# High and low parts of x side by side in one 512 column matmul, in passes of 256 output columns

## What is computed

```python
n = rmsnorm(h)                       # 256 x 2048
u = n @ w_in                         # A 6144, B 6144, C 10304 columns, gates 6144
# A: b * conv3(c * hid)              each 2048 wide
# B: stick-breaking attention        16 heads of 128, q, k, v
# C: z, xbc, dt = split(u_c); xbc = silu(conv4(xbc) + bias)
#    xdt = x * dt; W = exp(min(cs_l - cs_s, 0)) * (c b) lower half; y = W xdt + exp(cs) * c * state
#    y = (y + d * x) * silu(z); y = y * rsqrt(mean(y*y over a group)) * norm_w
h = h + (g_a*(y_a@w_a) + g_b*(y_b@w_b) + g_c*(y_c@w_c)) @ w_out
h = h + experts(rmsnorm(h))          # 16 of 16384 single-neuron experts for each of 8 heads
return rmsnorm(h, final_norm_w)
```

## Time and profile before

| | us |
|---|---|
| median of 3 runs | 3534.88 (3530.73 to 3535.65) |
| the profiled execution | 3526.34 |
| its span in the trace | 3524.6 |
| mean granted clock of PE | 0.997 |
| PE busy | 98% of the span |
| VectorE, ScalarE busy | 64%, 49% |
| start | 0 to 18.1 |
| A, its branch stage | 18.1 to 310.6, to 494.0 |
| B, its branch stage | to 812.9, to 993.0 |
| C, its branch stage | to 1512.0, to 1791.6 |
| output projection | to 1898.3 |
| expert stages | to 3512, end 3524.6 |

### The profile page before, as it was taken

How to read it: one execution, slowest core, us unless ns; L and a number is a source line. 1 busy time by engine, 2 the same in 40 slices (tenths; PEclk the granted TensorE clock), 3 DMA queues, 4 the chain that set the end, 5 groups by cost and what they waited for, 6 DMA issues and landing times.

```text
span 3524.6 us, 69345 instructions
## 1 busy us (share of the span) xinstructions
PE 3442.4 (98%) x23037; PEld 3164.8 (90%) x23037; DVE 2254.7 (64%) x2944; ACT 1717.8 (49%) x2494; POOL 26.3 (1%) x32
## 2 busy tenths in 40 slices
PE   8999999999999999999989999999999999999998
PEld 7999889998899999978879999999999988888887
DVE  4555444444547777774545998988889855554555
ACT  4444434444445455454435444447777644444444
POOL 0000000000000000000000000000000000000000
PEclk9999999999999999999999999999999999999999
DMA  6666665556666556556668576665666677667765
GB/s 179 175 176 176 187 179 157 158 157 178 193 188 189 174 168 186 172 155 194 188 190 209 158 171 177 175 175 160 158 160 159 166 195 192 193 193 219 197 192 166
DMA packets 484120, 628.63 MB, mean 178 GB/s; under 512 B 76832, under 2 KB 341504, under 8 KB 481792
## 3 DMA queue, kind: packets, MB, share of 16 engines
q1 hardware_dynamic: 483648, 626.51, 65.0%
q10 hardware_dynamic: 320, 0.08, 0.0%
HBM read 622.03 MB, written 4.26 MB: 178 GB/s over the span
## 4 chain that ended last, share of the span: by engine, by line
PE 81%; DVE 7%; DMA 4%; issue 3%; ACT 3%; SPq 2%; DVEq 0%; ACTq 0%
PE bank L81 26%; PE bank L82 25%; PE bank L83 25%; DMA w_raw<-in_peer_down 2%; DVE f_lo L128 2%; PE bank L1766 2%; PE bank L2176 2%; DVE w_lo L1617 1%; DVE c_xc L1200 1%; DMA f_raw<-in_w_in 1%; ACT f_hi L123 1%; SPq L458 1%; SPq L552 1%; DMA f_raw<-in_w_out 0%; SPq L465 0%
## 5 line engine op out<-in xcount | busy, mean ns | idle before, releaser
L128 DVE TENSOR_TENSOR f_lo<-f_raw,f_hi 128x768 fp32r<-128x768 f32 (+2 forms) x640 | 748.5, 1173 | 716.8 <-ACT f_hi L123 716.2
L123 ACT ACTIVATE f_hi<-f_raw 128x768 fp32r<-128x768 f32 (+2 forms) x640 | 646.2, 1016 | 752.1 <-DMA f_raw<-in_w_in 505.7
L81 PE MATMUL bank<-xT_hi,f_hi 128*128 128x256 f32 x2560 | 738.7, 289 | 26.9 <-DVE f_lo L128 12.0
L82 PE MATMUL bank<-xT_lo,f_hi 128*128 128x256 f32 x2560 | 723.9, 283 | 0.0
L83 PE MATMUL bank<-xT_hi,f_lo 128*128 128x256 f32 x2560 | 723.9, 283 | 0.0
L81 PE MATMUL bank<-xT_hi,w_hi 128*128 128x256 f32 x2048 | 587.4, 287 | 9.8 <-DVE w_lo L1617 9.6
L82 PE MATMUL bank<-xT_lo,w_hi 128*128 128x256 f32 x2048 | 579.1, 283 | 0.0
L83 PE MATMUL bank<-xT_hi,w_lo 128*128 128x256 f32 x2048 | 579.1, 283 | 0.0
L1704 DVE TENSOR_TENSOR w_lo<-w_raw,w_hi 128x1024 fp32r<-128x1024 f32 x256 | 313.7, 1225 | 340.1 <-PE bank L83 333.1
L81 PEld LDWEIGHTS bank<-xT_hi,f_hi 128*128 128x128 f32 x2560 | 490.2, 191 | 42.1 <-DVE f_lo L128 15.6
L82 PEld LDWEIGHTS bank<-xT_lo,f_hi 128*128 128x128 f32 x2560 | 490.5, 192 | 1.9 <-issue 1.7
(11 more groups left out here) (274 smaller groups left out, 4833.4 us busy)
## 6 DMA issues: line engine op xcount, KB each, us to landing
w_raw<-in_peer_down SPq DMA_DIRECT2D x1024, 128.0 KB, 3.4
w_raw<-in_peer_up SPq DMA_DIRECT2D x1024, 128.0 KB, 2.6
f_raw<-in_w_in SPq DMA_DIRECT2D x1024, 96.0 KB, 2.4
f_raw<-in_w_in SPq DMA_DIRECT2D x256, 256.0 KB, 2.9
f_raw<-in_w_in SPq DMA_DIRECT2D x384, 128.0 KB, 2.8
f_raw<-in_w_branch_c SPq DMA_DIRECT2D x256, 128.0 KB, 2.8
f_raw<-in_w_branch_a SPq DMA_DIRECT2D x128, 128.0 KB, 2.8
f_raw<-in_w_branch_b SPq DMA_DIRECT2D x128, 128.0 KB, 2.8
```

The source lines that it names most:

```text
L81: nc.tensor.matmul(out, lhs[0], rhs[0], start=start, stop=False, skip_group_check=True)
L82: nc.tensor.matmul(out, lhs[0], rhs[1], start=False, stop=False, skip_group_check=True)
L123: nc.scalar.activation(self.hi[u % 4][:, 0:cols], self.raw[u % 4][:, 0:cols], ACT.Copy).then_inc(self.hi_done, 1)
L128: nc.vector.tensor_tensor(self.lo[u % 4][:, 0:cols], self.raw[u % 4][:, 0:cols], self.hi[u % 4][:, 0:cols].bitcast(F32), ALU.subtract).the ...
```

## The change

**Operands.** `xT_hi` and `xT_lo` become the two halves of one tile `xT` [128, 2, 16, 256]. `pair_matmul` takes the place of `tri_matmul` in A, C and for q and k in B: one matmul of the high weights with 512 moving columns (256 of x high, 256 of x low) into a whole bank, then one of the low weights with the 256 high columns into the bank's first half. The result of 128 output columns is the sum of the two halves. The v part of B keeps its three matmuls.

**Passes.** A unit is now 4 contraction blocks x 256 columns (a 128 x 1024 slot), and four units make a pass: 256 finished output columns in two banks (`pass_unit`, 16 matmuls). A and B have 12 units an iteration (3 passes), C has 20 (x, x, B and C, z, z). `pass_load` issues four DMAs of 32 partitions, in runs of 1 KB (in pass 2 of C two for B, two for C, in runs of 512 B); SP's ring rules are as before.

**Sums.** Two units behind the end of a pass ScalarE copies the second halves of its banks out (`part_a`, `part_qk`, `part_c`), one unit later VectorE adds the first halves (`sum_a`, `sum_qk`, `sum_c`). PE waits for these sums before it starts a pass in the same banks. Passes use banks 0 to 5 in A, 0 to 3 (and 4 for v) in B, and in C 4, 2, 3, 0, 1 in turn.

**Steps moved.** In C the convolution of a group is made within its own iteration, its first tap by ScalarE (`taps`); the clamp min(., 0) goes from VectorE (8 instructions an iteration) to ScalarE (16 of 128 x 128, as a Relu of the negative, on which `exp_w` works in one instruction for a chunk); `xc` is doubled, and the loop over C covers two iterations. The steps stand so ("n" is the iteration's own group, others are of the one before, "r" of the one before that):

| step of C | before, unit | after, unit |
|---|---|---|
| ACT copies | 0 (five) | n: 6, 10, 14, 18; last pass: 2 (two each) |
| DVE sums | none | n: 7, 11, 15, 19; last pass: 3 |
| DVE convolution of block 0 to 5 | 0 to 5 | n: 9, 10, 13, 14, 17, 18 (ACT taps n: 8, 12, 16) |
| ACT silu of x, of z | 6, 7 | 0, 4 |
| clamp, first and second chunk | DVE 10, 12 | ACT n: 17; 1 |
| exponent of cs; of the weights (ACT) | 9; 10, 12 | n: 19; 5 |
| DVE tokens (`c_xdt`, `c_xdd`, `c_cbm`) | 8 | 4 |
| DVE weights | 12, 13 | 6 |
| PE turn, states, outputs | 6, 12, 13 | 0, 4, 8 |
| DVE skip and gate; fold | 15; r: 0 | 12; 15 |
| PE `square_sum` | r: 1 | 14 |
| DVE normalise; low part of y | r: 6; 7 | r: 0; 7 |
| SP `cs_load` | 4, of the group before | 13, of its own |

The rest follows from this: x is turned for six block pairs, not two, before unit 0 of A; unit u < 4 of the first iteration waits for the low part of x's blocks 4u to 4u+3; in the branch stages the accumulators use other bank pairs, the dt step bank 3, and in B's the low part of the last heads waits in a few places for `b_olo`. The text of the output projection and the expert stages stays, save for a semaphore that takes over another's counts.

```diff
+A_PASS = ((1, 0, 1), (2, 2, 3), (0, 4, 5))
+C_BANK = (4, 2, 3, 0, 1, 4, 2, 3, 0, 1)
...
-        xT_hi = sb(top, "xT_hi", [P, KD, T], F32R)
-        xT_lo = sb(top, "xT_lo", [P, KD, T], F32R)
+        xT = sb(top, "xT", [P, 2, KD, T], F32R)
+        xT_hi, xT_lo = xT[:, 0, :, :], xT[:, 1, :, :]
+
+        def pair_matmul(out, lhs, k, start, stop):
+            both = out[:, :].rearrange("p (s t) -> p s t", s=2)
+            nc.tensor.matmul(both, lhs[0], xT[:, :, k, :], start=start, stop=False, skip_group_check=True)
+            return nc.tensor.matmul(both[:, 0, :], lhs[1], xT_hi[:, k, :], start=False, stop=stop,
+                                    skip_group_check=True)
...
-        A_N, B_N, C_N = 128, 128, 128
+        A_N, B_N, C_N = 96, 96, 160
...
-        W, UN, N_IT = 1280, 16, GROUPS
+        W, UN, N_IT = 1024, 20, GROUPS
         zs = place("c_zs", [P, 4, T], at_s)
-        xc = place("c_xc", [P, 6, T], at_s + 4096)
+        xc = (place("c_xc0", [P, 6, T], at_s + 4096), place("c_xc1", [P, 6, T], at_s + 43648))
...
+                def pass_load(n, i, cols, rows):
+                    for q in (3, 2, 1, 0):
+                        at = slice(32 * q, 32 * q + 32)
+                        sp.dma_start(fl.raw[i][at, 0:1024].rearrange("p (k n) -> p k n", k=4)[:, :, cols],
+                                     rows.rearrange("(k p) n -> p k n", p=P)[at, :, :]).then_inc(fl.raw_full[i], 16)
...
-                def evacuate_a(p):
-                    act.wait_ge(fl.used, U_AB * p + U_AB)
-                    nc.scalar.activation(c_sb[:, :], bank[1][:, :], ACT.Copy).then_inc(a_evac, 1)
-                    nc.scalar.activation(b_sb[:, :], bank[0][:, :], ACT.Copy).then_inc(a_evac, 1)
+                def part_a(p, r):
+                    act.wait_ge(fl.used, U_AB * p + 4 * r + 4)
+                    for j in range(2):
+                        dst = (c_sb[:, j * T:(j + 1) * T], gate_hid[:, j, 2:T + 2], b_sb[:, j * T:(j + 1) * T])[r]
+                        if r == 1 and first_p(p) and j == 0:
+                            act.wait_ge(a_pad, 1)
+                        nc.scalar.activation(dst, bank[A_PASS[r][1 + j]][:, T:2 * T], ACT.Copy).then_inc(a_part, 1)
...
+                def taps(p, e, b):
+                    for j in (b, b + 1):
+                        act.wait_ge(ssd["evac"], 10 * p + j + 1)
+                        ch = 4 * p + j if j < 4 else (32 + p if j == 4 else 40 + p)
+                        nc.scalar.activation(xc[e][:, j, :], xpad[:, j, 3:T + 3], ACT.Identity,
+                                             bias=vcols[:, ds(V_CONVB + ch, 1)],
+                                             scale=vcols[:, ds(V_SSDW + 144 + ch, 1)]).then_inc(ssd["tap"], 1)
...
+                def clamp(p, ch):
+                    act.wait_ge(ssd["cs_in"], 16 * p + 16)
+                    if ch:
+                        act.wait_ge(ssd["ecs"], p + 1)
+                    for h in range(HPG):
+                        here = wts[:, ch, h, :]
+                        nc.scalar.activation(here, here, ACT.Relu, bias=cs_col[:, ch, ds(HPG * p + h, 1)],
+                                             scale=-1.0).then_inc(ssd["clamp"], 1)
+
                 def exp_w(p, ch):
-                    for q in range(2):
-                        act.wait_ge(ssd["min"], 4 * p + 2 * ch + q + 1)
-                        here = wts[:, ch, 4 * q:4 * q + 4, :]
-                        nc.scalar.activation(here, here, ACT.Exp).then_inc(ssd["exp"], 1)
+                    act.wait_ge(ssd["clamp"], 2 * HPG * p + HPG * (ch + 1))
+                    nc.scalar.activation(wts[:, ch, :, :], wts[:, ch, :, :], ACT.Exp, scale=-1.0).then_inc(ssd["exp"], 1)
...
+                        if u == 18:
+                            inv_rms(p)
...
+                def sum_a(p, r):
+                    for j in range(2):
+                        here = (c_sb[:, j * T:(j + 1) * T], gate_hid[:, j, 2:T + 2], b_sb[:, j * T:(j + 1) * T])[r]
+                        dve.wait_ge(a_part, 6 * p + 2 * r + j + 1)
+                        nc.vector.tensor_tensor(here, here, bank[A_PASS[r][1 + j]][:, 0:T], ALU.add).then_inc(a_sum, 1)
...
+                def sum_c(p, r):
+                    for j in (2 * r, 2 * r + 1):
+                        here = xpad[:, j, 3:T + 3] if r < 3 else zs[:, j - 6, :]
+                        dve.wait_ge(ssd["part"], 10 * p + j + 1)
+                        nc.vector.tensor_tensor(here, here, bank[C_BANK[j]][:, 0:T], ALU.add).then_inc(ssd["evac"], 1)
...
+                        if u == 15:
+                            fold(p)
...
+                def pass_unit(i, banks):
+                    for kk in range(4):
+                        k = 4 * i + kk
+                        for b in range(2):
+                            at = slice(kk * 256 + b * P, kk * 256 + b * P + P)
+                            last = pair_matmul(banks[b], (fl.hi[i][:, at], fl.lo[i][:, at]), k,
+                                               start=k == 0, stop=k == KD - 1)
+                    last.then_inc(fl.used, 1)
+
                 def a_unit(it, u, begin):
+                    r = u // 4
                     fl.wait_unit(pe, U_AB * it + u)
-                    for m in (2, 3, 0, 1, 4, 5):
-                        if u == 0 and not begin:
-                            if m == 2:
-                                pe.wait_ge(a_evac, 2 * it - 1)
-                            if m == 0:
-                                pe.wait_ge(a_evac, 2 * it)
-                            if m == 4:
-                                pe.wait_ge(a_gh, it)
-                        at = slice(m * P, (m + 1) * P)
-                        last = tri_matmul(bank[m // 2][:, (m % 2) * T:(m % 2 + 1) * T],
-                                          (fl.hi[u % 4][:, at], fl.lo[u % 4][:, at]), (xT_hi[:, u, :], xT_lo[:, u, :]),
-                                          start=u == 0 and m % 2 == 0, stop=u == KD - 1)
-                    last.then_inc(fl.used, 1)
+                    if u % 4 == 0 and not begin:
+                        pe.wait_ge(a_sum, 6 * it - 6 + 2 * r + 2)
+                    pass_unit(u % 4, (bank[A_PASS[r][1]], bank[A_PASS[r][2]]))
...
+                    if u % 4 == 0:
+                        if r >= 2:
+                            pe.wait_ge(ssd["evac"], 10 * it + (2, 4, 6)[r - 2])
+                        elif not begin:
+                            pe.wait_ge(ssd["evac"], 10 * it - 2 + 2 * r)
+                    pass_unit(u % 4, (bank[C_BANK[2 * r]], bank[C_BANK[2 * r + 1]]))
+
+                def ssd_step(p, e, u):
+                    if u == 0:
+                        turn(p, 1 - e)
+                    if u == 4:
                         states(p)
-                    if u == 13:
+                    if u == 8:
                         outputs(p)
+                    if u == 14:
+                        square_sum(p)
```

More of the change, by code:

```diff
@@ L142, in program @@
         O0 = GC0 + 96
+        first_p = lambda p: isinstance(p, int) and p == 0
         xt = place("xt", [P, TB, D], at_y)
@@ L263, in program @@
         ssd = {n: sem("c_" + n) for n in (
-            "pad", "evac", "conv", "xc", "tr", "btok", "cbm", "xdt", "cs_in", "sub", "min", "exp", "wts",
+            "pad", "part", "evac", "tap", "conv", "xc", "tr", "btok", "cbm", "xdt", "cs_in", "clamp", "exp", "wts",
             "zs", "cs", "ecs", "prev", "ce", "y", "skip", "yz", "sq", "fold", "sum", "rs", "yn", "yhi", "ylo")}
-        first_p = lambda p: isinstance(p, int) and p == 0
         o_tr = sem("o_tr")
@@ L1135, in copy_v, with sum_qk @@
                     nc.vector.tensor_copy(v_sb[:, :, :], V[:, :].rearrange("p (s d) -> p s d", s=TB)).then_inc(b_v, 1)
+                def sum_qk(p, r):
+                    for j in range(2):
+                        here = (q_sb, k_sb)[r][:, j, :]
+                        dve.wait_ge(b_part, 4 * p + 2 * r + j + 1)
+                        nc.vector.scalar_tensor_tensor(out=here, in0=(Q, K_)[r][j][:, 0:T], scalar=(SCALE, 1.0)[r],
+                                                       in1=here, op0=ALU.mult, op1=ALU.add).then_inc(b_qk, 1)
                 def softplus(p):
@@ L1994, in _ @@
                 pe.wait_ge(p_scaled, 1)
-                for pair in range(5):
+                for pair in range(6):
                     if pair == 4:
```

618 lines of the change are left out of this document (306 added, 312 removed).

## The result

| | before | after |
|---|---|---|
| median, us | 3534.6 (3530.7 to 3535.7) | 3498.0 (3490.8 to 3503.4) |
| profiled execution; span | 3526.3; 3524.6 | 3503.4; 3501.7 |

The ratio is 0.9902 (95% interval 0.989 to 0.9915): 36.5 us faster at the medians, where 70 were forecast. The value lies in the stated range, but the change brought half of what it was said to bring.

A forecast was written before the change was run, and what follows sets the result against it. PE was taken to set the pace in A, B and C. Savings of 21.3 (A), 15.4 (B), 25.4 (C), 7 (branch stage after C) and 1 (other branch stages) sum to 70 us: 3534.9 - 70 = 3465 us, range 3440 to 3503.

The forecast's parts named there:

- the supply in C: Loads and splits feeding C's units: path 7.3 us at worst against 8.3 of PE work, slack growing to 1.0 us.
- The upper bound of 4 us per iteration: C: upper bound on two new waits, column sum and loads held up by `cs_load`; 0.7 us was booked.
- The clock: Branch stage after C: granted clock averaging 0.91 in 1540 to 1560 costs 1.8 us; would return to 1.00.
- Rival 1: Matmuls of A, B, C: the pair wins nothing on PE; price 36 us, time 3501, chance 0.11.
- Rival 2: ScalarE and VectorE queues late: C waits 4 instead of 0.7 us an iteration; price 28, time 3493, chance 0.13.
- The column sum's wait: C: `square_sum` after unit 14 waits for VectorE's fold behind unit 15's low part, about 0.5 us late.
- The pair: A, B (q, k), C: two matmuls take 0.346 us for three's 0.360; 2560 x 0.014 = 36 us saved.
- The turn of an iteration: PE's wait for accumulator copies goes: 0.85 us, 7 times each in A, B and C, C's 0.94 with it.
- the four issues still take about 2.2: SP's load issues for a unit take about 2.2 us against 2.77 of PE, so SP stops being tight.

The follow-up runs named there:

- the 64 KB kernel: The changed kernel with the 1 MB `cs_load` of C reduced to 64 KB from the second group on; ratio 0.9831 to the kernel before.
- the eight small loads: The changed kernel with two tiles of decay weights used in turn and `cs_load` cut into eight of 128 KB across C's iteration; ratio 0.988 to the kernel before.
- the kernel with three matmuls: The changed kernel with three matmuls of 256 columns in place of each pair, all else kept; ratio 0.9983 to the kernel before.

## Why the forecast was wrong, step by step

**The failed step is the supply in C.** The forecast worked out a unit's way (7.3 us) against three units of PE work (8.3) from loads that land in 3.4 us, and booked "0.2 us for loads held up by the 1 MB `cs_load`, now in a stage with less slack". The chain held in A and B, the term did not: the load costs 3.6 to 3.7 us an iteration, 25 to 26 in the seven that were measured and 29 for all eight at that price, because the last of the loads behind it lands after 6.1 to 8.8 and not 3.4 us. It could have been worked out from rows of before. The slack was 8.3 - 7.3 = 1.0 us. A's row has 177 GB/s at 0.66 busy, which is 268 GB/s for full engines with runs of 1 KB. By that, an estimate, 1 MB keeps the engines for 3.9 us; less the slack, 2.9 us of wait are left in each of eight iterations, 23 us. C would have been forecast at 494 + 23 = 517 us, and the total at 3488. (It is also slow to be made good: the weights of the new units ask 185, the full engines moved 232, so 47 GB/s are spare.) Before, three units were 10.8 us, 2.5 more than now. The load had stood there without a wait, and I took this for its price. The upper bound of 4 us per iteration was written down and was near; the value chosen between the bounds was not worked out.

**The clock.** The forecast saw the lower level in the stage after C, and there it did go (0.91 in the earlier trace rows, 0.99 for the whole stage before and 1.00 now; 6.5 saved of 7). It did not ask what new waits of 3 us do to it in C: some 10 of the 29 us are matmuls behind the waits.

**Rivals 1 (3501) and 2 (3493) came near the measured 3498 by luck, and both are wrong in cause.** Rival 2 put 3.3 us per iteration on the queues of ScalarE and VectorE. The loss is 3.6 to 3.7, but those queues are as full in the 64 KB kernel, which has none of it from the second group on. The column sum's wait, booked at 0.5, is there: it hides behind the large wait and shows once this is gone (with the eight small loads 1.0 to 1.1 us from start to start in six of the eight groups, 5.7 us lost in all).

**The pair.** 0.346 was forecast, 0.3467 and 0.3533 are measured, 0.3505 on the mean: 2560 x 0.0095 = 24 us instead of 36. Rival 1 (nothing won) is refuted by the kernel with three matmuls, and the estimate by the Trainium skill, 2560 x 0.0025 = 6 us ("TensorE: Matmul & The Clock Gate", section "Back-to-back issue gap"), with it. In A this is 768 x 0.0073 = 5.6 us, just what A fell short (16.0 for 21.3). B was in the short kind and without a wait: 38.13 us an iteration for 38.25 forecast, and its first one 33.8 for 35.7.

**The turn of an iteration** went as forecast in A and B, and nothing took its place. The first iteration of A took 37.5 us for 37.7. SP did not come free in all passes, as "the four issues still take about 2.2" had it: in pass 2 of C they take 3.2 (0.78 each, 512 B runs over 64 partitions), more than the unit.

**The sum.** Of the missing 47 us in the profile, C is 34.7 (some 29 the load, 5 to 6 the pair), A 5.3 the pair, the expert stages 11.3 (chance or not, the profiles don't tell for sure); B gives 2.8 back, the other stages 1.4. With the load in smaller pieces, its own tile, the sum two units later and SP's loop written out, the change is worth 61 us.

## What to carry to other kernels

When a unit of work gets shorter, the ring in front of it covers less time by the same share, and every transfer beside the stream must be priced again, in bytes that the DMA engines have to spare within the cover, not by the wait it caused before. A burst is not cured by cutting it where it stands; it wants a destination that is free early, so that it can be spread. And a wait hides the ones behind it: take the first away in an experiment before booking what is left.

## What the runs showed of the hardware

- A 512 column matmul and a 256 column one in turn start 0.3467 or 0.3533 us apart, with the same operands; the stream keeps one of the two over hundreds of pairs and changes only at a pause or another instruction.
- A branch back over a loop body of two C iterations left SP without an instruction for 2.9 to 3.8 us (four branches, two kernels), one over a single iteration for 0.2; written out in a row, SP had no such gap.
- PE's branch back over a body of two C iterations lasted 4.3 to 5.6 us in nine cases of 22, else 0.2. At each of the nine, two 16 KB packets on one of the trace's instruction queues start within 1.5 us of it (1203.9 and 1204.2 for the branch at 1202.8); within 6 us of the thirteen short ones there are none.
- In the changed kernel's loop a load of 64 partitions in 512 B runs (256 runs) takes SP 0.60 us of busy time to issue, one of 32 partitions in 1 KB runs (128 runs) 0.32; written out, 0.62 and 0.43.
- Right behind the 1 MB load, in 1195 to 1200, the full DMA engines moved runs of 1 KB at 232 GB/s; A's share and rate would have given 268.
- A wait of 2 to 3 us did not always cost the clock: of the eight in C, six (2.3 to 4.7 us) were followed by the lower level, those of 2.9 and 2.2 us were not.
